# Lows-last projections at four places, two reordered steps on ScalarE and VectorE, and the last two output tiles in two token halves

## The reference

```
h = first_block(x, ...)        # attention + gated convolution mixer, then conv-gated MLP (d_ff 2816)
x = ssd_gla_layer(h, ...)      # 16 SSD heads and 8 GLA heads side by side, one output projection
x = moba_layer(x, ...)         # attention with 16 heads, sigmoid-gated (silu) output
out = rms_norm_2(x, final_norm)
    # y = x * rsqrt(mean(x*x over the 1024 channels) + eps);  out = y * w
```

## Time and profile before

| | |
|---|---|
| median of 3 runs | 842.08 us (841.49 to 842.10) |
| the profiled execution's own time | 841.78 us |
| its span, first to last instruction | 839.9 us |
| granted TensorE clock, mean of the core | 0.999 |
| TensorE's matmuls | 829.0 us busy, 6768 passes |
| VectorE, ScalarE, GpSimd busy | 623.8, 504.9, 122.3 us |

### The profile page before, as it was taken

The page is one execution under the profiler, slowest core; times in us unless marked ns, Lnnn a source line. Parts: engine busy times, 40 slices in busy tenths (PEclk is TensorE's granted clock), DMA queues, the critical chain, the costliest instruction groups (busy, mean ns, idle before and its releaser), DMA issues.

```text
span 839.9 us, 16864 instructions
## 1 busy us (share of the span) xinstructions
PE 829.0 (99%) x6768; PEld 799.6 (95%) x6768; DVE 623.8 (74%) x1055; ACT 504.9 (60%) x876; POOL 122.3 (15%) x119
## 2 busy tenths in 40 slices
PE   9999999999999999999999999999999999999997
PEld 8999999999999999999999999989999999888896
DVE  6647888886666688676664478999989696568765
ACT  6446567555444567555554368787878555356655
POOL 1000000000000305434441100042415010000002
PEclk9999999999999999999999999999999999999999
DMA  8744434345555436555565525545455365553331
GB/s 290 279 164 140 145 105 171 128 142 176 185 181 188 170 102 206 192 190 180 188 197 193 182 98 164 196 141 177 156 170 169 107 228 187 187 173 129 127 101 51
DMA packets 39853, 139.81 MB, mean 166 GB/s; under 512 B 4432, under 2 KB 5088, under 8 KB 39648
## 3 DMA queue, kind: packets, MB, share of 16 engines
q1 hardware_dynamic: 38160, 135.90, 48.8%
q10 hardware_dynamic: 1616, 2.84, 1.1%
HBM read 137.65 MB, written 1.06 MB: 165 GB/s over the span
## 4 chain that ended last, share of the span: by engine, by line
PE 84%; DVE 8%; ACT 4%; issue 1%; DMA 1%; POOL 1%; SPq 0%; DVEq 0%; ACTq 0%; POOLq 0%
PE ps L1802 68%; PE ps L1849 4%; PE ps L1805 4%; DVE weights_lo L1071 2%; ACT weights_hi L543 1%; PE ps L1974 1%; PE ps L1959 1%; PE ps L1988 1%; PE ps L2243 1%; DMA raw_weights<-weights_in 1%; PE ps L2261 1%; DVE arena L1382 1%; PE ps L2251 1%; POOL arena L477 0%; DVE arena L1327 0%
## 5 line engine op out<-in xcount | busy, mean ns | idle before, releaser
L1071 DVE TENSOR_TENSOR weights_lo<-raw_weights,weights_hi 128x1024 fp32r<-128x1024 f32 x251 | 313.0, 1251 | 81.5 <-ACT weights_hi L543 81.4
L1802 PE MATMUL ps<-x_hi,weights_hi 128*128 128x256 f32 (+3 forms) x1224 | 354.0, 289 | 1.1 <-DVE weights_lo L1071 0.8
L543 ACT ACTIVATE weights_hi<-raw_weights 128x1024 fp32r<-128x1024 f32 x251 | 263.2, 1053 | 145.6 <-PE ps L1802 61.4
L1802 PE MATMUL ps<-x_lo,weights_hi 128*128 128x256 f32 (+3 forms) x1224 | 345.4, 282 | 0.0
L1802 PE MATMUL ps<-x_hi,weights_lo 128*128 128x256 f32 (+3 forms) x1224 | 344.8, 282 | 0.0
L1802 PEld LDWEIGHTS ps<-x_hi,weights_hi 128*128 128x128 f32 x1224 | 230.7, 188 | 7.9 <-issue 6.0
L1802 PEld LDWEIGHTS ps<-x_lo,weights_hi 128*128 128x128 f32 x1224 | 230.7, 188 | 0.7 <-issue 0.5
L1802 PEld LDWEIGHTS ps<-x_hi,weights_lo 128*128 128x128 f32 x1224 | 231.1, 189 | 0.0
L1802 PE MATMUL ps<-y_hi,weights_hi 128*128 128x256 f32 (+1 forms) x488 | 137.8, 282 | 0.0
L1802 PE MATMUL ps<-y_lo,weights_hi 128*128 128x256 f32 (+1 forms) x488 | 137.6, 282 | 0.0
L1802 PE MATMUL ps<-y_hi,weights_lo 128*128 128x256 f32 (+1 forms) x488 | 137.3, 281 | 0.0
(11 more groups left out here) (274 smaller groups left out, 1131.1 us busy)
## 6 DMA issues: line engine op xcount, KB each, us to landing
raw_weights<-weights_in SPq DMA_DIRECT2D x251, 512.0 KB, 3.7
arena<-decay_rows ACTq DMA_DIRECT2D x8, 256.0 KB, 4.0
masks<-masks_in SPq DMA_DIRECT2D x1, 1186.0 KB, 8.4
raw_weights<-weights_in SPq DMA_DIRECT2D x4, 256.0 KB, 4.3
hidden<-xT_in SPq DMA_DIRECT2D x3, 272.0 KB, 4.8
hidden<-xT_in SPq DMA_DIRECT2D x1, 276.0 KB, 3.1
gate_w<-gate_w_in ACTq DMA_DIRECT2D x1, 256.0 KB, 3.7
out<-arena ACTq DMA_DIRECT2D x1, 256.0 KB, 2.1
```

The lines of the kernel that those rows point to most:

```text
L543: a.sig(A(whi[:, s * CW:(s + 1) * CW], raw[:, (c % RAW) * CW:(c % RAW + 1) * CW], ACT.Copy), "hi_ready")
L1071: d.sig(TT(wlo[:, s * CW:(s + 1) * CW], raw[:, (c % RAW) * CW:(c % RAW + 1) * CW], whi[:, s * CW:(s + 1) * CW].bitcast(F32), ALU.subtract) ...
L1802: ins = mm(bank(BANK_OF[no])[:, 0:b - a], wt, x_[:, kt, a:b], start=s0, stop=s1)
```

## The change

It has these parts:

1. ScalarE makes the high part of chunk 2 in two halves, and chunk 3's between the two squares of x; VectorE makes the low parts of chunks 2 and 3 before the sum of squares. `first_keys` goes block by block in its second and fourth quarters. ("k", 2) begins on the first half of its chunk, and ("k", 4) is made with `project_lows_last`.
2. "fu" and "fg" 4 and 5 are made with `project_lows_last` too.
3. `project_lows_last` takes tiles of several chunks and with tokens on partitions, and makes ("ev", 1).
4. `gla_squares(1)` moves on ScalarE from after `feed(("ek", 2))` to before `gla_exps(2)`.
5. ("mo", 6) and ("mo", 7) are made in two halves of 128 tokens, in the order (6, half 0), (7, half 0), (6, half 1), (7, half 1), each with 24 passes of 128 columns. Residual, square, gained copy and the last steps of GpSimd's sum are by halves. The sum over the partitions of half 0 stands before the last block of (6, half 1). VectorE multiplies the first four tiles of half 0 before the residual of (7, half 1), and the rest after it. The five stores are cut anew.

```diff
-        STORES = ((0, 0, 2), (0, 2, 5), (0, 5, KT), (1, 0, 4), (1, 4, KT))
+        STORES = ((0, 0, 4), (0, 4, KT), (1, 0, 2), (1, 2, 5), (1, 5, KT))
...
@@ GpSimd, end
-            add_squares(6 * KT, META)
+            for i in range(1, KT - 2):
+                pool.wait_ge(S("sq_ready"), 6 * KT + i + 1)
+                g.settle()
+                g.step(nc.gpsimd.tensor_tensor(sq[:, 0, META:T], sq[:, 0, META:T], sq[:, i, META:T], ALU.add))
+            for c in range(2):
+                w_ = slice(META + P * c, META + P * c + P)
+                pool.wait_ge(S("sq_ready"), 7 * KT - 2 + c + 1)
+                g.settle()
+                g.sig(nc.gpsimd.tensor_tensor(sq[:, 0, w_], sq[:, 0, w_], sq[:, KT - 2, w_], ALU.add), "sq_summed")
...
@@ ScalarE, start
-            nxt[0] = 2
-            split_hi()
+            half_high(2, 0)
+            half_high(2, 1)
+            nxt[0] = 3
             for n in range(2):
                 a.sig(A(sq[:, 4 * n:4 * n + 4, 0:T], H[:, 4 * n:4 * n + 4, 0:T], ACT.Square), "sq_ready", 4)
-            split_hi()
+                if n == 0:
+                    split_hi()
...
@@ ScalarE, SSD and GLA
                 else:
-                    gla_squares(p - 1)
+                    if p == 3:
+                        gla_squares(2)
                     feed(("ev", p))
...
                     tap(("ex", u + 3), u + 3, xs[:, u + 3, :])
+                    if p == 1:
+                        gla_squares(1)
                     gla_exps(p + 1)
...
@@ ScalarE, end
-            for i in range(KT - 1):
+            for i in range(KT - 2):
                 feed(("mo", i))
...
-            feed(("mo", KT - 1))
+            for i in (KT - 2, KT - 1):
+                feed(("mo", i))
+
+            def half_squares(i, c):
+                w_ = slice(META + P * c, META + P * c + P)
+                act.wait_ge(S("half_sum"), 2 * c + i - (KT - 2) + 1)
+                a.sig(A(sq[:, i, w_], H[:, i, w_], ACT.Square), "sq_last" if i == KT - 1 else "sq_ready")
+                if i == KT - 2:
+                    a.sig(A(fin[:, c, i, :], H[:, i, w_], ACT.Copy, scale=pcol("final_norm", i)), "gained")
+
             for c in range(2):
                 w_ = slice(META + P * c, META + P * c + P)
-                act.wait_ge(S("h_ready"), 3 * KT + KT + c)
-                a.sig(A(sq[:, KT - 1, w_], H[:, KT - 1, w_], ACT.Square), "sq_ready")
-            for c in range(2):
-                w_ = slice(META + P * c, META + P * c + P)
+                half_squares(KT - 2, c)
+                half_squares(KT - 1, c)
                 inverse_rms(rinv[:, w_], P, D, 8 + c, bank((SSB, 6)[c])[:, 0:P])
...
@@ VectorE, start
             nxt[0] = 2
             split_lo()
+            split_lo()
...
-            square_sum(0, 0, split_lo)
+            square_sum(0, 0)
...
@@ VectorE, end
+            def half_residual(i, c):
+                w_ = slice(META + P * c, META + P * c + P)
+                r = (bank(4 + i % 2) if c else bank(BANK_OF[FIRST_OUT["mo", i]]))[:, 0:P]
+                dve.wait_ge(S("half_out"), 2 * c + i - (KT - 2) + 1)
+                d.sig(TT(H[:, i, w_], r, H[:, i, w_], ALU.add), "half_sum")
+                if i == KT - 1:
+                    d.settle()
+                    d.step(TS(fin[:, c, i, :], H[:, i, w_], pcol("final_norm", i), None, ALU.mult))
+
+            def finish(n):
+                c, i0, i1 = STORES[n]
+                rc = rL[:, P * c:P * c + P].unsqueeze(1).to_broadcast([P, i1 - i0, P])
+                dve.wait_ge(S("gained"), KT - 1 + c)
+                dve.wait_ge(S("rms_ready"), 8 + c)
+                d.settle()
+                d.sig(TT(fin[:, c, i0:i1, :], fin[:, c, i0:i1, :], rc, ALU.mult), "final")
+
+            half_residual(KT - 2, 0)
+            half_residual(KT - 1, 0)
+            half_residual(KT - 2, 1)
+            finish(0)
+            half_residual(KT - 1, 1)
+            finish(1)
+            for n in (2, 3, 4):
+                finish(n)
...
@@ TensorE
-            def project_lows_last(tile, hi, lo, a, b, ready=None):
+            def project_lows_last(tile, hi, lo, a, b, ready=None, toks=None, begin="hi_ready"):
...
+                for j0 in range(0, nb, BPC):
+                    c = (f + j0) // BPC
+                    pe.wait_ge(S(begin), c + 1)
+                    for j in range(j0, j0 + BPC, step):
+                        if ready is not None:
+                            ready(j // step)
+                        passes(whi, hi, j, j == 0, False)
+                        passes(whi, lo, j, False, False)
+                    pe.wait_ge(S("lo_ready"), c + 1)
+                    for j in range(j0, j0 + BPC, step):
+                        done = passes(wlo, hi, j, False, j + step >= nb)
...
@@ first_keys, quarters 1 and 3 (0 and 2 keep their order)
+                        for kt in kts:
+                            for c in range(2):
+                                part(c, kt, whi, xhi, "x_hi")
+                                part(c, kt, wlo, xhi, "x_hi")
+                        for kt in kts:
+                            for c in range(2):
+                                ins = part(c, kt, whi, xlo, "x_split", kt == KT - 1)
...
-            project_lows_last(("k", 2), xhi, xlo, 0, T)
+            project_lows_last(("k", 2), xhi, xlo, 0, T, second_half, begin="hi_half")
             project_lows_last(("k", 3), xhi, xlo, 0, T)
-            project(("k", 4), xhi, xlo, 0, T, first_total)
+            project_lows_last(("k", 4), xhi, xlo, 0, T, first_total)
...
-                up = project_lows_last if i < 4 else project
+                up = project_lows_last if i < 6 else project
...
-                    project(("ev", 1), xhi, xlo, META, T, toks=toksL)
+                    project_lows_last(("ev", 1), xhi, xlo, META, T, toks=toksL)
...
+            def project_half(i, c, ready=None):
+                ch = FIRST_BLOCK["mo", i] // BPC
+                b_ = bank(4 + i % 2) if c else bank(BANK_OF[FIRST_OUT["mo", i]])
+                if c == 0:
+                    bank_free(FIRST_OUT["mo", i])
+                pe.wait_ge(S("lo_ready"), ch + 1)
+                for kt in range(KT):
+                    if ready is not None:
+                        ready(kt)
+                    at = (ch % RING) * CW + kt * P
+                    for n, (w_, x_) in enumerate(((whi, ehi), (whi, elo), (wlo, ehi))):
+                        ins = mm(b_[:, 0:P], w_[:, at:at + P], x_[:, kt, P * c:P * c + P],
+                                 start=kt == 0 and n == 0, stop=kt == KT - 1 and n == 2)
+                ins.then_inc(S("half_out"), 1)
+
+            def half_sums(c):
+                w_ = slice(META + P * c, META + P * c + P)
+                pe.wait_ge(S("sq_summed"), 4 + c)
+                mm(bank((SSB, 6)[c])[:, 0:P], ones, sq[:, 0, w_], start=True, stop=False)
+                pe.wait_ge(S("sq_last"), c + 1)
+                mm(bank((SSB, 6)[c])[:, 0:P], ones, sq[:, KT - 1, w_], start=False, stop=True).then_inc(
+                    S("sums_ready"), 1)
+
+            for i in range(together, KT - 2):
+                project(("mo", i), ehi, elo, 0, L)
+            project_half(KT - 2, 0)
+            project_half(KT - 1, 0)
+            project_half(KT - 2, 1, lambda kt: half_sums(0) if kt == KT - 1 else None)
+            project_half(KT - 1, 1)
+            half_sums(1)
```

More of the change, by code:

```diff
@@ L1810, in project, with passes @@
                         ins.then_inc(S("chunk_read"), 1)
-            def project_lows_last(tile, hi, lo, a, b, ready=None):
+            def project_lows_last(tile, hi, lo, a, b, ready=None, toks=None, begin="hi_ready"):
                 f, nb, no = FIRST_BLOCK[tile], BLOCKS_OF[tile], FIRST_OUT[tile]
[L1815 to L1827, removed]
-                    ins = mm(dst, wlo[:, at:at + P], hi[:, kt, a:b], start=False, stop=kt == KT - 1)
-                ins.then_inc(S("out_ready"), 1)
+                assert f % BPC == 0 and nb % BPC == 0
+                for o in range(OUTS_OF[tile]):
+                    bank_free(no + o)
+                step = 1 if toks is None else nb // KT
+                outs = [None] if toks is None else toks
+                def passes(w_, part, j, s0, s1):
+                    at = ((f + j) // BPC % RING) * CW + (j % BPC) * P
+                    w, kt, done = w_[:, at:at + step * P], j // step, []
+                    for o, tok in enumerate(outs):
+                        if tok is None:
+                            done.append(mm(bank(BANK_OF[no])[:, 0:b - a], w, part[:, kt, a:b], start=s0, stop=s1))
+                        else:
+                            t0, t1 = tok
+                            done.append(mm(bank(BANK_OF[no + o])[0:t1 - t0, 0:step * P], part[:, kt, t0:t1], w,
+                                           start=s0, stop=s1))
+                    return done
+                for j0 in range(0, nb, BPC):
[9 more added lines that the diff above has]
```

(28 more changed lines are left out.)

48 lines of the change are left out of this document (13 added, 35 removed).

## The result

| | before | after |
|---|---|---|
| median | 841.9 us (841.49 to 842.10, 6 runs) | 844.88 us (844.46 to 845.17, 6 runs) |
| ratio, 95% interval | | 1.0036 [1.0026, 1.0045] |
| span of the profiled execution | 839.9 us | 842.8 us |
| its own time | 841.78 us | 844.91 us |

A forecast was written before the change was run, and what follows sets the result against it. TensorE, busy 829.0 of 839.9 us, was taken as the bound. The terms -1.05 - 0.45 - 0 - 0.35 + 4.0 = +2.15 us, added to 842.08, gave 844.2 us, range 842.6 to 845.4.

The forecast's parts named there:

- Part A: First keys: ("k", 2) starts 0.35 us sooner and the 0.70 us stall before ("k", 4) goes; gain 1.05 us.
- Part B: ("fu", 4) to ("fg", 5) with low passes last: the wait before ("fu", 4) goes; gain 0.45 us, bounds 0.3 to 0.45.
- Part C: ("ev", 1) with low passes last: the 0.67 us gained returns as a wait in ssd_heads(3); gain 0, bounds 0 to 0.7.
- Rival 2: The gaps at ("ev", 1) and the moved squaring are kept in full, 0.7 + 0.65 us more: 842.8 us; chance 0.12.
- Part D: gla_squares(1) ahead of gla_exps(2): TensorE gains about 1.05 us, ssd_heads(7) eats the rest; gain 0.35 us, bounds 0 to 1.0.
- Part E: Last two tiles in halves: weight loads at 0.110 us cost TensorE 5.3 us, the tail saves 1.3; loss 4.0 us.
- rival 1: In the 96 half-tile matmuls, columns, not loads, set the cadence, 0.065 us: 4.3 us less, 839.9 us; chance 0.08.
- The first half's finish: At the end, it gets in the way of the second's, so the 1.3 us isn't won: 845.5 us; chance 0.10.

The follow-up runs named there:

- e3_keys_mlp: The kernel before with only the first keys and the MLP tiles ("fu", "fg") changed: 840.38 us against 842.26 before, ratio 0.9980.
- e5: The kernel before with only ("ev", 1) made with low passes last: 841.82 us against 841.97 before, ratio 0.9999.
- e11: The changed kernel with the old end, plus GpSimd's ssd_weights(5) ahead of ssd_add(3): 840.24 us against 841.99 for the kernel before, ratio 0.9979.
- e7: The changed kernel, its last two multiplications no longer waiting for the one before: 844.55 us against 841.97 for the kernel before, ratio 1.0029.
- e1_tail_only: The kernel before with only the last two tiles made in halves: 846.76 us against 842.26 before, ratio 1.0053.
- e6: The changed kernel with each pass of the halves cut into two of 64 columns: 873.09 us against 841.97 for the kernel before, ratio 1.0369.
- e8_pool_order: The changed kernel with the old end, plus GpSimd's ssd_weights(2p+1) ahead of ssd_add(2p-1) at all three pairs: 841.82 us against 841.97 for the kernel before.

## Why the prediction was right, and where its terms were off

**The bound.** TensorE's stream was the bound, and the time is the sum of its matmuls and gaps: the shifts read in its timeline add up to the whole difference.

**Part A, -1.05 forecast.** In the profiled pair the first matmul behind ("v", 1) comes 0.96 us earlier (37.02 against 37.98), of which ("k", 4) has 0.85. The start of ("k", 2) gave 0.15 instead of 0.35, the stall its 0.70. Hardly any of this rests on the first wait of the span: behind it, at 11.05 us, the two kernels are within 0.03 us.

**Part B, -0.45.** At ("fu", 4) the shift grows from 1.02 us (322.61 against 323.63) to 1.50 (323.54 against 325.04): 0.48, the forecast gain. By 493 us it is 1.58; this last 0.1, above the upper bound of 0.45, was not followed. A and B together were forecast at 1.50; in the trace they are 1.58, and e3_keys_mlp has 1.9 with the interval 1.0 to 2.4.

**Part C, 0.** Right, and by its reason: the shift grows to 2.23 us at ("ev", 1) and is back at 1.53 at ssd_heads(3). The wait there grew to 0.7 us (0.9 was forecast), because GpSimd's product was no earlier than its own chain let it be, and e5 shows it alone. Rival 2 falls with it.

**Part D, -0.35.** This step failed. It said that ScalarE is 0.5 us shorter and VectorE could follow by about 0.35. The squaring fitted, and TensorE gained the forecast 1.05 us at the sum; but nothing was kept. 0.3 us went by 602.18; the runs do not show why. Then, once shifted, GpSimd's addition and products fall beside other VectorE work and take 0.80 and 0.82 us more, which eats 0.69 us in ssd_heads(5); the kernel stands at 1.57 us ahead, as if D were not there. The prediction placed the loss in ssd_heads(7); it is in ssd_heads(5). It took GpSimd's durations as fixed, and they are not. e11 shows that even without it ssd_heads(7) would have taken the rest, so the lower bound, 0, was the right value for both reasons.

**Part E, +4.0.** The cadence was 0.110 forecast and 0.112 measured; the term for TensorE was +5.3 and is +5.46. The prediction inferred it from starts of loads and said that no row shows such a stream. The kernel before has one, in gla_out (timeline of the kernel before):

```profile
588.43 1.05 PE L2146 MATMUL ps<-arena 128*128 128x128 f32 x8
589.32 0.83 PE L2149 MATMUL ps<-arena 128*128 128x128 f32 x6
```

These are plain float32 passes (four matmuls in the code, eight passes), so another form, but each with a load of 128 columns and 128 columns moving: eight of them from 588.43 to 589.32 are 0.111 us apart. That row gave the price of the halves before any run, and it spoke against rival 1. The tail behind the last matmul gave 1.05 instead of 1.3: the three last multiplications took 1.81 us (838.64), not 1.3 to 1.4, because `finish` waits before each for the one before. e7 removes two of these waits and gets 1.36 us. The prediction counted what is multiplied and missed the wait between. That is 0.45 us; 0.2 came back elsewhere, for the steps behind the last multiplication are 0.25 us shorter, where 0.1 was forecast, and the chain ahead of the multiplications is 0.05 shorter. Together E is +4.4 instead of +4.0; e1_tail_only has 4.5 with the interval 3.3 to 5.6, and its trace, 4.9 us longer in span, of which 0.5 us stands ahead of the tail, has 4.4.

**The rivals.** Columns do not set the cadence at 128 (0.112) nor at 64 (e6). The first half's finish does not get in the way: its rms is through at 834.4 and its second multiplication (837.38) lies in the wait for the second half's.

**The sum.** -0.96 - 0.62 + 0.07 + 4.4 = +2.9 in the profiled pair, where 0.07 is what C and D moved; +2.98 in the medians. Of the 0.8 us by which the forecast fell short, D has 0.4 and E 0.4; A and B brought 0.1 more than forecast, and 0.1 is between the medians and the profiled pair. The forecast was right in direction, bound and main term, and its two misses added up instead of cancelling.

## What to carry to other kernels

With 64 to 256 moving columns, count a matmul that keeps 128 stationary columns by its weight load (here 0.112 us, and 0.118 at 256), not by the columns that move. Cutting a moving side of 256 in two nearly doubles its price, and what it saves behind the last matmul must be more than that. Look for a stream of the same shape in the kernel that you have before you infer its cadence. A wait removed from the bounding engine is a gain only if the chain that feeds the next joint moves too, so follow the feeding engines to that joint before booking anything. In that chain GpSimd and VectorE operations on SBUF operands got in each other's way, so a shift of about a microsecond changed durations that the forecast took as fixed.

## What the runs showed of the hardware that was not expected

- A stream of 64-column matmuls, each with a load of 128 columns, ran at a granted TensorE clock of 1.00 at first and of 0.50 (1.2 instead of 2.4 GHz) from 828.6 us on, though the engine never stood still; passes went from 0.112 to 0.213 us. With 128-column matmuls at the same cadence it stayed at 1.00 through both tiles.
- In e8_pool_order the granted clock went to 0.50 for 3.4 us just after TensorE had stood still for 1.35 and 0.18 us, and passes of 256 columns went from 0.118 to 0.213 us: TensorE lost 1.5 us by it, about as much as by the waits themselves.
- Two VectorE products of 128x256 took 2.34 us instead of 0.76 beside GpSimd's products, and four final multiplications 3.03 instead of about 1.93, all of it in the one that started just after GpSimd's; GpSimd's 128x256 addition took 1.54 instead of 0.74, its pair of 128x384 products 3.00 instead of 2.18.
